# A hybrid retention / delta-rule / expert-retrieval block on one core: slots chosen in smaller first groups and later, one query half block per pair of slots, the second norm's factor applied at evictions, first loads in another order

## The reference

```python
def reference(x, ...):
        h = _rmsnorm(x, ln1_w[l])
        proj = (h @ w_in[l]).astype(f32)
        ...
        o_r = _retention(q_r, k_r, _heads(rv, RET_HEADS))
        ...
        o_g = _gated_delta_rule(q_g, k_g, _heads(cv, GDN_HEADS),
                                g_dec.transpose(0, 2, 1), beta.transpose(0, 2, 1))
        ...
        x = x + mixed @ w_out[l]
        h2 = _rmsnorm(x, ln2_w[l])
        x = x + _peer(h2, peer_wq[l], peer_keys[l], peer_u[l], peer_v[l])
    return _rmsnorm(x, lnf_w)

def _peer(h, wq, sub_keys, u_tab, v_tab):
        q = (xb @ wq).reshape(PEER_BLOCK, PEER_HEADS, 2, PEER_HALF)
        s = jnp.einsum('thpd,hpkd->thpk', q, sub_keys).astype(jnp.float32)
        s1, i1 = lax.top_k(s[:, :, 0], PEER_TOPK)
        s2, i2 = lax.top_k(s[:, :, 1], PEER_TOPK)
        ...
        best, pos = lax.top_k(cand, PEER_TOPK)
        ids = jnp.take_along_axis(cid, pos, axis=-1).reshape(PEER_BLOCK, -1)
        gate = jax.nn.softmax(best, axis=-1).reshape(PEER_BLOCK, -1)
        act = jax.nn.gelu(jnp.einsum('tkd,td->tk', u_tab[ids], xb).astype(jnp.float32), approximate=False)
        return jnp.einsum('tk,tkd->td', (gate * act).astype(xb.dtype), v_tab[ids])
```

## Time and profile before

| | |
|---|---|
| median of 3 executions | 3158.55 us (3156.93 to 3163.96) |
| the profiled execution, its own time | 3163.53 us |
| its span | 3161.7 us |
| TensorE busy | 76% of the span |
| VectorE busy | 65% |
| ScalarE, POOL busy | 37% each |
| mean DMA rate | 400 GB/s, 1265.77 MB |
| indirect transfers | 1024, 1073.81 MB |

### The profile page before, as it was taken

How to read it: one execution, slowest core, us unless ns; L and a number is a source line. 1 busy time by engine, 2 the same in 40 slices (tenths; PEclk the granted TensorE clock), 3 DMA queues, 4 the chain that set the end, 5 groups by cost and what they waited for, 6 DMA issues and landing times.

```text
span 3161.7 us, 36216 instructions
## 1 busy us (share of the span) xinstructions
PE 2399.0 (76%) x12496; PEld 1393.2 (44%) x12496; DVE 2058.1 (65%) x5319; ACT 1173.6 (37%) x3422; POOL 1156.2 (37%) x1030
## 2 busy tenths in 40 slices
PE   8877778987775778996775678897778478765555
PEld 7754456754441345762452245664345134421111
DVE  4375945678479854668649874667846976486444
ACT  2233433353434433344323533425333443233222
POOL 0033322335333433334325443333433444244442
PEclk9998888999986999998997799898998788876787
DMA  8399989999999999999999999999999999999997
GB/s 341 121 387 420 407 339 371 410 420 419 420 406 420 419 415 419 414 421 419 404 419 400 420 419 421 415 418 420 419 418 380 420 419 420 420 412 420 420 420 321
DMA packets 177591, 1265.77 MB, mean 400 GB/s; under 512 B 21504, under 2 KB 21632, under 8 KB 24960
## 3 DMA queue, kind: packets, MB, share of 16 engines
q0 software_dynamic: 147456, 1073.81, 82.4%
q1 hardware_dynamic: 28224, 183.72, 14.2%
q10 hardware_dynamic: 1728, 5.94, 0.5%
HBM read 1259.19 MB, written 4.19 MB: 400 GB/s over the span
## 4 chain that ended last, share of the span: by engine, by line
PE 38%; DMA 36%; DVE 14%; ACT 6%; issue 3%; POOL 3%; SPq 0%; ACTq 0%; POOLq 0%; DVEq 0%
DMA uv<-uv_tab,ids 30%; PE y_ps L468 13%; PE bank L525 11%; PE bank L517 7%; DVE uv L1147 6%; DMA wbuf<-w 6%; POOL uv L444 3%; PE bank L532 2%; ACT diag L839 1%; PE y_ps L547 1%; DVE area L1210 1%; PE bank L492 1%; ACT actT L867 1%; DVE arena L1491 1%; PE bank L782 1%
## 5 line engine op out<-in xcount | busy, mean ns | idle before, releaser
L444 POOL DMA_INDIRECT uv<-uv_tab,ids x1024 | 1155.7, 1129 | 1972.2 <-PE y_ps L468 1632.9
L1147 DVE CUSTOM_DVE_ANT_0 uv<-uv,h 128x1024 f32<-128x1024 f32 x1024 | 1240.8, 1224 | 817.6 <-DMA uv<-uv_tab,ids 811.0
L468 PE MATMUL y_ps<-uv,diag 128*64 128x512 f32 x4096 | 1190.0, 714 | 517.9 <-ACT diag L839 493.0
L468 PEld LDWEIGHTS y_ps<-uv,diag 128*64 128x64 f32 x4096 | 288.9, 155 | 1186.0 <-ACT diag L839 709.6
L833 ACT ACTIVATE gelu<-dots 128x2 f32<-128x2 f32 x512 | 104.1, 203 | 1383.9 <-DVE dots L1147 1383.5
L525 PE MATMUL bank<-actT,wbuf 128*128 128x128 f32 x2688 | 347.1, 292 | 52.2 <-DMA wbuf<-w 47.6
L525 PEld LDWEIGHTS bank<-actT,wbuf 128*128 128x128 f32 x2688 | 333.3, 206 | 106.8 <-issue 66.8
L839 ACT ACTIVATE diag<-gated,gelu 128x64 f32<-128x64 f32 x1024 | 300.7, 340 | 64.1 <-PE y_ps L468 5.4
L829 ACT ACTIVATE gated<-smalls,gate 128x64 f32<-128x64 f32 x1024 | 294.2, 336 | 13.6 <-DVE acc L1161 13.6
L517 PE MATMUL bank<-wbuf,actT 128*128 128x256 f32 x960 | 232.0, 397 | 33.5 <-DMA wbuf<-w 22.6
L517 PEld LDWEIGHTS bank<-wbuf,actT 128*128 128x128 f32 x960 | 184.6, 197 | 100.9 <-issue 35.1
(11 more groups left out here) (216 smaller groups left out, 1863.8 us busy)
## 6 DMA issues: line engine op xcount, KB each, us to landing
wbuf<-w SPq DMA_DIRECT2D x146, 1024.0 KB, 9.4
uv<-w SPq DMA_DIRECT2D x20, 1024.0 KB, 21.8
uv<-uv_tab,ids POOLq DMA_INDIRECT x1024, 16.8
acc<-x SPq DMA_DIRECT2D x8, 512.0 KB, 13.0
y<-acc ACTq DMA_DIRECT2D x8, 512.0 KB, 7.9
rowbuf<-x SPq DMA_DIRECT2D x5, 512.0 KB, 5.8
actT_ahead<-x SPq DMA_DIRECT2D x3, 512.0 KB, 18.0
keys_sb<-keysT ACTq DMA_DIRECT2D x1, 1024.0 KB, 14.2
```

The source lines that it names most:

```text
L444: nc.gpsimd.indirect_dma_start(out=uv[i % RING][:, :, :].rearrange("p z d -> p (z d)"), out_offset=None, in_=uv_tab, in_offset=bass.Indire ...
L468: done = mm(y_ps[z][64 * j:64 * j + 64, :], diag[:, i % DIAGS, :], uv[i % RING][:, 1, 512 * z:512 * z + 512], start=(s % PAIRS == 0), stop ...
L1147: V.tensor_tensor_reduce(out=u, in0=u, in1=h2[n % 2][:, j, :], scale=1.0, scalar=0.0, op0=ALU.mult, op1=ALU.add, accum_out=dots[:, i % DOT ...
```

## The change

The first groups become smaller and the windows start later. The query blocks q2 and q3 get one pair each between their half blocks. TensorE transposes `acc` itself; the factor of the second norm (`rstd2`) goes into the evictions of scores and replicated rows. `ids` are written and signalled before the gates are weighed. The identity, the norm weights and two weight blocks are loaded before the other constants. One Sqrt on a spare cell is added in chunk 0.

```diff
-GROUPS = [[(0, 1), (1, 2), (2, 4), (4, PH)] if n == 0 else [(0, 4), (4, PH)] for n in range(NCH)]
+GROUPS = [[(0, 1), (1, 2), (2, 4), (4, PH)] if n == 0 else [(0, 2), (2, 4), (4, PH)] if n < 3 else [(0, 3), (3, PH)]
+          for n in range(NCH)]
...
-WINDOW = {"first": (20, 10), "second": (15, 5), "alone": (17, 7), None: (15, 5)}
+WINDOW = {"first": (16, 14), "second": (12, 8), None: (12, 8)}
...
-    if n < 2:
-        return ((-3, 22), (48, 76))[n]
+    if n < 3:
+        return ((-3, 22), (55, 83), (118, 138))[n]
     before, after = WINDOW[KIND[n + 1] if n + 1 < NCH else None]
     return PAIRS * n - before, PAIRS * n + after
+
+
+def length(n):
+    return window(n)[1] - window(n)[0]
...
             sp.dma_start(rowbuf[:, :], x[0]).then_inc(x_loaded, 16)
-            for dst, src in ((tab[:, :, :], tables), (lnT[:, :, :], cols[:, 0:2 * KT].rearrange("p (z k) -> p z k", z=2)),
-                             (w_ab_sb[:, :, :], w_ab), (headsb[:, :], head_rows.partition_broadcast(P)),
-                             (conv_w[:, :, :], cols[:, 2 * KT:2 * KT + 48].rearrange("p (c j) -> p c j", j=4)),
-                             (normw[:, :], cols[:, 2 * KT + 48:])):
-                sp.dma_start(dst, src).then_inc(const_in, 16)
-
+            sp.dma_start(ident, tables[:, 0, :]).then_inc(first_in, 16)
+            sp.dma_start(lnT[:, :, :], cols[:, 0:2 * KT].rearrange("p (z k) -> p z k", z=2)).then_inc(first_in, 16)
             loads = [0]
 
             def weights(blocks):
@@ -407,6 +409,12 @@
                     into, loaded = weight_home(k)
                     sp.dma_start(into, w[b]).then_inc(loaded, 16)
 
+            weights(range(2))
+            for dst, src in ((w_ab_sb[:, :, :], w_ab), (headsb[:, :], head_rows.partition_broadcast(P)),
+                             (conv_w[:, :, :], cols[:, 2 * KT:2 * KT + 48].rearrange("p (c j) -> p c j", j=4)),
+                             (tab[:, 1:, :], tables[:, 1:, :]), (normw[:, :], cols[:, 2 * KT + 48:])):
+                sp.dma_start(dst, src).then_inc(const_in, 16)
+
...
                 if c.kind != "second":
-                    weights(range(IN_BLOCKS))
+                    weights(range(2 if n == 0 else 0, IN_BLOCKS))
...
                 if n + 1 < NCH and KIND[n + 1] != "second":
-                    sp.wait_ge(*event("h2T", n, 1))
+                    sp.wait_ge(*event("ss2", n))
...
-            pe.wait_ge(const_in, 16 * N_CONST)
+            pe.wait_ge(first_in, 16 * N_FIRST)
...
-                at(0.22)
+                at(0.22 if n < 2 else 0.26)
...
-                at(0.25)
+                first = 0.25 if n < 2 else 0.29
+                at(first)
...
-                pe.wait_ge(*event("x2_norm", n))
                 for j in range(2):
-                    if n == 0 and j == 1:
-                        pe.wait_ge(other_half, 2)
-                    transposes(n, f"h2T{j}", lambda i: rowbuf[:, P * (4 * j + i):P * (4 * j + i) + P], 4)
+                    pe.wait_ge(*event("x2", n, j))
+                    transposes(n, f"h2T{j}", lambda i: acc[n % 2][:, P * (4 * j + i):P * (4 * j + i) + P], 4)
...
-                    steps = iter((0.02, 0.04, 0.06, 0.08))
+                    steps = iter(range(1, 5))
                     for j in (2, 3):
-                        project(n, f"q{j}", cols_product, [actT], lambda: at(next(steps)))
+                        project(n, f"q{j}", cols_product, [actT], lambda: at(next(steps) / length(n)))
                     sub_scores(n, (2, 3))
-                    at(0.11)
+                    at(5 / length(n))
                     replicate(n)
...
                     if group_of(n, pair) is not None:
-                        act.wait_ge(routed, chosen(n, group_of(n, pair)))
+                        act.wait_ge(weighed, chosen(n, group_of(n, pair)))
...
                 if n == 0:
...
-                at(0.23)
+                    act.wait_ge(first_in, 16 * N_FIRST)
+                first = 0.25 if n < 2 else 0.29
+                at(first - 0.02)
...
+                if n == 0:
+                    for dst, src in ((ret_qdec[:, :, :], qdec), (smalls[:, :], small),
+                                     (keys_sb[:, :, :], keysT), (lnf_row[:, :], rows.partition_broadcast(P))):
+                        act.dma_start(dst, src).then_inc(late_in, 16)
+                    act.wait_ge(const_in, 16 * N_CONST)
+                    A(exp_a[:, :], a_log, ACT.Exp).then_inc(start_up, 1)
+
...
                 put("vnew", "vnew", vnew[:, :, :], c)
+                if n == 0:
+                    A(st[:, 84:85], eps_col[:, 0:1], ACT.Sqrt)
                 turn()
...
+                for j in range(2 if n > 0 else 1):
+                    columns("h2T", f"h2T{j}", lambda i: actT[:, 4 * j + i, :],
+                            lambda i: lnT[:, 1, 4 * j + i:4 * j + i + 1], c)
+                turn()
                 act.wait_ge(*event("x2", n, 1))
                 A(rowbuf[:, :], acc[n % 2][:, :], ACT.Square, accum_out=st[:, 0:1]).then_inc(S["ss2"], 1)
                 act.wait_ge(*event("ss2", n))
                 A(st[:, 1:2], st[:, 0:1], ACT.Sqrt, bias=eps_col[:, 0:1], scale=1.0 / D).then_inc(S["sqrt2"], 1)
-                turn()
-                act.wait_ge(*event("rstd2", n))
-                mine = slice(0, D // 2 if n == 0 else D)
-                A(rowbuf[:, mine], acc[n % 2][:, mine], ACT.Copy, scale=st[:, 2:3]).then_inc(S["x2_norm"], 1)
                 if n == 0:
                     act.wait_ge(late_in, 16 * N_LATE)
                 turn()
-                for j in range(2 if n > 0 else 1):
-                    columns("h2T", f"h2T{j}", lambda i: actT[:, 4 * j + i, :],
-                            lambda i: lnT[:, 1, 4 * j + i:4 * j + i + 1], c)
                 turn()
                 turn()
                 if n == 0:
                     two(c, "first_q", "q0a", qT[:, 0:2, :])
-                    two(c, "first_s", "s0a", scores[:, 0:2, :])
+                    act.wait_ge(*event("rstd2", 0))
+                    two(c, "first_s", "s0a", scores[:, 0:2, :], rstd2)
                     turn()
                     turn()
                     return
@@ -1066,16 +1077,17 @@
...
             def put_scores(c, j):
-                put("scores", f"s{j}", scores[:, 4 * j:4 * j + 4, :], c)
+                act.wait_ge(*event("rstd2", c.n))
+                put("scores", f"s{j}", scores[:, 4 * j:4 * j + 4, :], c, scale=rstd2)
 
             def replicated(c):
                 for i in range(4):
-                    A(h2[c.n % 2][:, i // 2, 512 * (i % 2):512 * (i % 2) + 512], filled(act, f"rep{i}", c)[:, :], ACT.Copy
-                      ).then_inc(S["rep"], 1)
+                    A(h2[c.n % 2][:, i // 2, 512 * (i % 2):512 * (i % 2) + 512], filled(act, f"rep{i}", c)[:, :], ACT.Copy,
+                      scale=st[:, 86 + i // 2:87 + i // 2]).then_inc(S["rep"], 1)
...
-                waiting = [(0.40, 0), (0.90, 1)] if n > 0 else [(0.22, 1), (0.45, 2), (0.90, 3)] if n == 0 else []
+                waiting = [((a + 0.8 * (z - a)) / PH, g) for g, (a, z) in enumerate(GROUPS[n])] if n > 0 else []
+                if n == 0:
+                    waiting = [(0.22, 1), (0.45, 2), (0.90, 3)]
...
-                    at(0.04)
+                    at(2.3 / length(n))
                     put("qT", "q2", qT[:, 8:12, :], c)
-                    at(0.08)
+                    at(4.3 / length(n))
                     put("qT", "q3", qT[:, 12:16, :], c)
                     for j in (2, 3):
                         put_scores(c, j)
-                    at(0.12)
+                    at(5.5 / length(n))
                     replicated(c)
...
                 turn()
+                if n == 0:
+                    half_columns(1, "h2T1", "h2T")
+                turn()
+                turn()
                 dve.wait_ge(*event("sqrt2", n))
-                V.reciprocal(st[:, 2:3], st[:, 1:2]).then_inc(S["rstd2"], 1)
-                if n == 0:
-                    half_norm(1, "rstd2", x2, "h2T1", "h2T")
-                turn()
-                for _ in range(4):
+                V.reciprocal(rstd2, st[:, 1:2])
+                for j in range(2):
+                    for q in range(2):
+                        last = V.reciprocal(st[64 * q:64 * q + 64, 86 + j:87 + j], st[64 * j:64 * j + 64, 1:2])
+                last.then_inc(S["rstd2"], 1)
+                for _ in range(3):
                     turn()
...
-                        dve.wait_ge(*event("scores", n, z // 2 - 1))
+                        dve.wait_ge(*event("scores", n, (z + 1) // 2 - 1))
...
+                    here = slice(TOPK // 2 * a, TOPK // 2 * z)
+                    quarters = [(q, j, slice(64 * q, 64 * q + 64), slice(64 * j, 64 * j + 64)) for q in range(2) for j in range(2)]
+                    for q, j, into, of in quarters:
+                        places = [sel[of, part, mine].rearrange("p (s q) -> p q s", q=2)[:, q, :] for part in range(2)]
```

(23 more changed lines are left out.)

46 lines of the change are left out of this document (22 added, 24 removed).

## The result

The changed kernel took 3143.02 us in the median of 5 executions (3140.97 to 3145.10), the kernel before 3161.63 us in the median of 5 beside it: ratio 0.994, 95% interval 0.9928 to 0.9953. That is 18.6 us; forecast were 24.7, with a range of 3123 to 3145 us for the time, so that the result lies 2 us inside its upper end. The profiled execution took 3143.25 us, its span is 3141.3 us, 20.4 us under that of before.

The account below looks back on a forecast made before the run. The kernel was taken as bound by its transfers: 3014 us at 420 GB/s, 148 us stalled or slow. Gains 5.7 + 10 + 10 - 1 = 24.7 us gave a 3134 us median, range 3123 to 3145 us.

Parts of the forecast that it names:

- First slots: Chain before POOL's first issue at 144.16 us: first slots come 5.7 us earlier, bounds 4.2 and 6.9.
- First loads: Kernel start: TensorE awaits only the identity and norm weights, so the first product starts 1.5 us earlier.
- Norm: Second norm of chunk 0: transposes of `acc` end at 121.6 instead of 124.8 us, gain 3.2 us.
- mix(1): Mixer spread over 33 pairs instead of 26: 10 us of its 14.9 us hole (418 to 470 us) go.
- The straight line between 26 and 39 pairs: Estimate for the mixer's hole: 8.0 us left at 33 pairs, a gain of 6.9 us.
- One pair per half block: Split q2 and q3 half blocks: gain 10 of the 11.1 us in two later holes; lower bound 5.5.
- with one pair between, the ring refills each time: At q2 and q3: pair and block need 7.5 us of transfer, TensorE 3.84 us plus the pair's matmuls.
- Window 1 unchanged: Hole at 525 to 550 us stays at 7.7 us; bounds 7.7 better and 7.7 worse.
- third rival: Hand-over between chunks: slots come too late, 17.5 us given back over 7 hand-overs, 3151 us; chance 0.07.
- More groups: Chunks 1 and 2 choose in three groups instead of two: 1 us worse, between 0 and 10.6.
- The holes move instead of closing: Where routing, replication and inputs meet, a new TensorE wait replaces the old; 3150 us, chance 0.17.
- TensorE at its low clock: Half blocks spread singly leave TensorE idle, so they run 2.65 us longer; 37 us in all, 3171 us; chance 0.05.

Follow-up runs that it names:

- e4: Kernel before with only the later windows 1 and 2 (mixer spread) and three groups in chunks 1 and 2; 3151.31 us, ratio 0.9963 to the kernel before.
- e1: Changed kernel with windows, groups and q2/q3 spacing of before, leaving start, norm, `ids` and early Sqrt; 3156.26 us, ratio 0.9981 to the kernel before.
- e3: Changed kernel with the q2/q3 spacing of before, keeping the new windows; 3149.08 us, ratio 0.9964 to the kernel before.
- e10: e9 with window 2 from 116 to 136 and two groups in chunk 2; 3132.32 us, ratio 0.9908 to the kernel before.
- e9: Changed kernel with ScalarE's evictions of q2, q3, replicated rows and transposed input rows one gelu earlier; 3132.31 us, ratio 0.9905 to the kernel before.
- e11: e10 with one pair between the gate products and the first half block of the inputs; 3132.32 us, ratio 0.9907 to the kernel before.
- e8: Changed kernel with only ScalarE's eviction of the transposed input rows earlier, 0.26 of the window instead of 0.27; 3136.06 us, ratio 0.9919 to the kernel before.
- e12: Changed kernel with 8 more 128-column matmuls ahead of each gate product in windows 1, 3 and 5; 3146.45 us, ratio 0.9955 to the kernel before.
- e2: Changed kernel with windows and groups of before, keeping one pair per half block; 3153.94 us, ratio 0.9970 to the kernel before.

## Why the prediction was right, and which steps were not

**Direction, time and bound** held: the bytes are the same, and the starts of windows 2, 4 and 6 now run at 420 GB/s, the rate that the sum goes by; none of the 40 slices of the changed kernel's page runs above it. That the time came out close is in part luck: errors of 11.4 us one way and 15.7 the other are in it, and they are named below. The range, 3123 to 3145 us, is not what its own bounds give: they add up to gains of 10.6 to 30.8 us, or 3128 to 3148 us, and the measured 3143.02 lies in both.

**First slots, 5.7 us**: 7.7. First loads 1.5: measured 1.55. Norm 3.2: 3.8, and 1.6 more that I had left out, the clock of the product behind it. `ids` 0.9: 0.7, less 0.2 lost. The early Sqrt and the rest of the mixer: 0.3 for 0.1.

**mix(1), 10 us**: 14.8 by place. The straight line between 26 and 39 pairs gave 6.9; e4 shows 14.2 for the spreading alone. The term was too small because the line between two mixers was, not because of the norm's wait that I added. By the view of waits TensorE waited 45.0 us in 8 times for these scaled rows before, and without them e1 gained some 6 us in all, most of it at the start.

**One pair per half block, 10 us**: 11.7 at the window starts, by e3's 17.0 against 4.5 rather 12.5. The step that failed is "with one pair between, the ring refills each time": it follows TensorE's half blocks and not the ScalarE eviction that each product ends in, so it knows no wait of 13 us. The rates came as I said (413 GB/s from place 39 to 50, 420 at the starts of windows 2, 4 and 6). POOL's waits there did not fall under 10 us as I said (12.30 us at 892.29, 13.52 at 2392.92); they are covered.

```profile
892.29 1.52 POOL L452 DMA_INDIRECT uv<-uv_tab,ids  x1 [12.30 <-PE y_ps L476]
...
2392.92 1.21 POOL L452 DMA_INDIRECT uv<-uv_tab,ids  x1 [13.52 <-PE y_ps L476]
```

**Window 1 unchanged**: 10.0 us before, 10.2 after, but by another cause. The old hole closed (e3: 2.7) and a new one opened, from the late q3 by way of the scores to `ids`:

```profile
524.11 2.08 PE L590 MATMUL bank<-keys_sb,arena 128*128 128x128 f32 x8 [8.27 <-ACT arena L869]
...
542.28 0.94 POOL L452 DMA_INDIRECT uv<-uv_tab,ids  x1 [9.46 <-DVE ids L1519]
```

This is the third rival's sign, POOL waiting for VectorE at the first pair of a chunk, in one chunk of seven.

**More groups, 1 us**: 4.1 us at the finish of chunk 1, by where chunk 2's last group starts, not by its instructions (e10).

**What I had not priced** are the 12.6 us of windows 3 and 5. "The holes move instead of closing" had 0.17 and the right mechanism, a new wait for TensorE where queries and inputs meet; it took 12.6 us back, where I had priced it at 24.7 - 8.7 = 16. "TensorE at its low clock" is not the cause: the lump's half block took 6.03 and 6.48 us, and 6.47 and 5.44 before. The errors nearly cancel: +2.0 start, +4.8 mixer, +1.7 blocks, +2.9 rest, against -12.6 and -3.1 (chunk 1's finish beside the 1 us), which leaves 20.4 of 24.7.

The kernel that beats both is e9: 0.9905 of before, with an interval (0.9890 to 0.9920) that does not touch the changed kernel's (0.9928 to 0.9953); e10 and e11 are no slower.

## What to carry to other kernels

When a step is moved on one engine, check in every other engine's program that the instruction it waits for is not now behind one more instruction that waits for a transfer; here a rounding of 0.3 pair cost a wait of 13 us. A wait is worth what it takes from the stock of transfers: 45 us of TensorE's waits went for little, while two evictions, each one gelu late, cost some 11 us. Where two causes share a hole, undo both before calling one of them wrong, and look whether the sign that you took for the cause was there before: the slow half block was.

## What the runs showed of the hardware that I had not expected

TensorE's granted clock fell from 1.00 to 0.50 while it was at work. In the changed kernel it did so at 1276 us, behind pauses of 4.12 and 0.90 us:

```profile
1274.00:1276.00 2.00, 1.89 (x18) 1.00 0.99 410
1276.00:1278.00 2.00, 2.00 (x13) 0.59 1.05 434
```

A pause right before is not needed. In e8 TensorE worked without one from 1263.37 us on, and the clock fell at 1273 us, at the end of the gate products; windows, then timeline:

```profile
1270.00:1272.00 2.00, 2.00 (x19) 1.00 1.03 426
1272.00:1274.00 2.00, 2.00 (x16) 0.76 1.02 422
1274.00:1276.00 2.00, 2.00 (x10) 0.50 1.01 418
```

```profile
1263.37 3.33 PE L476 MATMUL y_ps<-uv,diag 128*64 128x512 f32 x8 [6.33 <-ACT diag L847]
...
1274.85 6.21 PE L533 MATMUL bank<-actT,wbuf 128*128 128x128 f32 x32
```

In e12 it stayed at 0.50 for over 14 us of work without a gap. The Trainium skill, page "TensorE: Matmul & The Clock Gate", section "What's actually happening", says that the default is the throttled clock and activity releases it; by these rows the release can also be taken back in the middle of work. What decides it, these runs do not show.

Nor is the chain before the first pair, the same in e1, e2, e3 and the changed kernel, always as long: POOL's first issue came at 138.2, 136.5, 133.5 and 136.4 us, with a granted clock of 0.83, 0.83, 0.91 and 0.83 between 40 and 60 us.
